# Splitting the delta rule's output into stages and putting attention scores and projections between them

## The reference, cut to what matters

```python
def gated_delta_rule(q, k, v, g, beta):          # 4 heads of 128, run here on blocks of 128 tokens
    a_mat = strict_lower(kbeta @ k.T * decay) + I
    u, w = solve(a_mat, [v * beta, kbeta * exp(g)])
    attn = lower(q @ k.T * decay)
    for n in blocks:                             # state starts at 0
        v_new = u_n - w_n @ state
        o_n = (q_n * exp(g_n)) @ state + attn_n @ v_new
        state = state * exp(g_last) + (k_n * exp(g_last - g_n)).T @ v_new

o_a = rmsnorm(gated_delta_rule(...)) * silu(gz)
o_b = softmax(causal(qf @ kf.T * scale)) @ vm * silu(mz)      # 8 heads, 192 wide, two at a time
x = x + concat([o_a, o_b, o_c]) @ w_out
```

## Time and profile before

| what | value |
|---|---|
| median of three executions | 1759.2 us |
| profiled execution | 1756.48 us, span 1754.7 us |
| PE busy | 1661.3 us, 95% |
| VectorE busy | 1048.1 us, 60% |
| ScalarE busy | 872.9 us, 50% |
| mean granted TensorE clock | 0.974 of full |
| HBM traffic | 253.24 MB, 144 GB/s on average |

### The profile page before, as it was taken

The page is one execution under the profiler, slowest core; times in us unless marked ns, Lnnn a source line. Parts: engine busy times, 40 slices in busy tenths (PEclk is TensorE's granted clock), DMA queues, the critical chain, the costliest instruction groups (busy, mean ns, idle before and its releaser), DMA issues.

```text
span 1754.7 us, 27203 instructions
## 1 busy us (share of the span) xinstructions
PE 1661.3 (95%) x11578; PEld 1531.1 (87%) x11578; DVE 1048.1 (60%) x1506; ACT 872.9 (50%) x1297; POOL 97.7 (6%) x72
## 2 busy tenths in 40 slices
PE   7999899999989899999888999999999998789999
PEld 7989777989977799999887899989999997679998
DVE  6875564896646555555786645455646465555554
ACT  4975363686445435435445533344454357443332
POOL 0112000012200000000240000000000000000000
PEclk9999999999999899999999999998999999899999
DMA  7624224552313465555321555544665553035552
GB/s 224 191 66 135 71 73 145 157 158 89 97 49 117 163 213 191 171 190 169 121 83 62 168 186 179 188 140 135 196 204 175 185 169 120 24 113 179 190 192 97
DMA packets 204297, 253.24 MB, mean 144 GB/s; under 512 B 17808, under 2 KB 183952, under 8 KB 204048
## 3 DMA queue, kind: packets, MB, share of 16 engines
q1 hardware_dynamic: 204176, 251.49, 44.9%
HBM read 250.43 MB, written 1.05 MB: 143 GB/s over the span
## 4 chain that ended last, share of the span: by engine, by line
PE 78%; DVE 8%; ACT 6%; issue 5%; DMA 1%; POOL 1%; SPq 0%; DVEq 0%; ACTq 0%; POOLq 0%
PE bank L784 77%; ACT arena L1377 4%; DVE weights_rest L1889 2%; ACT weights_high L1377 1%; PE bank L842 1%; DVE arena L2036 1%; DMA ring<-in_w_in 1%; ACT L1377 1%; ACT L1372 1%; DVE small L2206 0%; DVE x L2252 0%; DVE weights_rest_more L1889 0%; DVE arena L2224 0%; POOL arena L2520 0%; DMA vec<-in_vec 0%
## 5 line engine op out<-in xcount | busy, mean ns | idle before, releaser
L784 PE MATMUL bank<-xT_high,weights_high 128*128 128x256 f32 (+1 forms) x2352 | 676.1, 288 | 8.9 <-DVE weights_rest L1889 4.1
L784 PE MATMUL bank<-xT_rest,weights_high 128*128 128x256 f32 (+1 forms) x2352 | 658.3, 284 | 0.0
L784 PE MATMUL bank<-xT_high,weights_rest 128*128 128x256 f32 (+1 forms) x2048 | 581.4, 285 | 0.0
L1889 DVE TENSOR_TENSOR weights_rest<-ring,weights_high 128x1024 fp32r<-128x1024 f32 (+3 forms) x414 | 486.6, 1225 | 98.8 <-ACT weights_high L1377 95.1
L1377 ACT ACTIVATE weights_high<-ring 128x1024 fp32r<-128x1024 f32 (+3 forms) x414 | 400.6, 1019 | 253.9 <-PE bank L784 235.6
L784 PEld LDWEIGHTS bank<-xT_high,weights_high 128*128 128x128 f32 (+1 forms) x2352 | 454.2, 193 | 19.4 <-issue 8.9
L784 PEld LDWEIGHTS bank<-xT_rest,weights_high 128*128 128x128 f32 (+1 forms) x2352 | 448.1, 192 | 3.5 <-issue 2.0
L784 PEld LDWEIGHTS bank<-xT_high,weights_rest 128*128 128x128 f32 (+1 forms) x2048 | 395.7, 193 | 0.6
L1377 ACT ACTIVATE arena<-bank 128x512 f32<-128x512 f32 (+4 forms) x253 | 134.5, 547 | 390.3 <-PE bank L784 327.4
L784 PE MATMUL bank<-arena 128*128 128x128 f32 (+2 forms) x1416 | 209.4, 307 | 37.3 <-ACT arena L1377 22.9
L784 PEld LDWEIGHTS bank<-arena 128*128 128x128 f32 (+1 forms) x1416 | 180.2, 203 | 63.6 <-ACT arena L1377 22.6
(11 more groups left out here) (180 smaller groups left out, 1698.1 us busy)
## 6 DMA issues: line engine op xcount, KB each, us to landing
ring<-in_w_in SPq DMA_DIRECT2D x36, 1024.0 KB, 5.2
ring<-in_ffn_w_gate SPq DMA_DIRECT2D x36, 1024.0 KB, 5.4
ring<-in_ffn_w_up SPq DMA_DIRECT2D x35, 1024.0 KB, 5.4
ring<-in_ffn_w_down SPq DMA_DIRECT2D x34, 1024.0 KB, 4.9
ring<-in_w_out SPq DMA_DIRECT2D x22, 1024.0 KB, 4.9
ring<-in_w_in_a SPq DMA_DIRECT2D x11, 1024.0 KB, 5.2
ring_more<-in_ffn_w_down SPq DMA_DIRECT2D x10, 1024.0 KB, 5.1
ring_more<-in_ffn_w_up SPq DMA_DIRECT2D x9, 1024.0 KB, 5.3
```

The source lines that it names most:

```text
L784: return eng.matmul(o, a, b, start=first, stop=last)
L1889: TTs(rest_slot(b)[:, part], raw_slot(b)[:, part], high_slot(key)[:, part].bitcast(F32), ALU.subtract).then_inc(*dv.mark(("rest", key, z)))
```

## The change

`gdn_o` is cut into four kinds of stages, and the scores of a pair get a stage `sc` of their own for pairs 0 and 1 (for these, `att` does nothing on PE and only the DVE part is left). The matmuls, evictions and products are the same ones in the same number.

- `gdn_u` l, n: PE u (for n = 1 also w); ACT their evictions.
- `gdn_w` l: PE wS; DVE the subtraction.
- `gdn_o` l, n: PE S (n = 0) and o; ACT the copy of S and the square of o; nothing on DVE.
- `gdn_n` l, n: PE on; ACT logarithm and exponential; DVE the products by norm, gain and gates.

The order in each layer becomes

The diff, cut to its core (the engines' functions are cut along the same lines; `LABEL` only keeps the semaphores' names):

```diff
+LABEL = dict(gdn_u="gdn_o", gdn_w="gdn_o", gdn_n="gdn_o", sc="att")
...
-                  32: (rots[0:3], rots[3:5]), 64: ([proj("mz", 0)], [])}
+                  32: (rots[0:3], rots[3:5]), 64: ([proj("mz", 0)], [("sc", f"m{l}", 0)])}
...
-        out += [("gdn_o", l, 0), ("att", m, 0), ("sm", m, 0), proj("mz", 1), ("gdn_o", l, 1)]
+        out += [("gdn_u", l, 0), ("att", m, 0), ("sm", m, 0), proj("mz", 1), ("gdn_o", l, 0), ("gdn_u", l, 1)]
+        out += [("sc", m, 1), ("gdn_n", l, 0), ("gdn_w", l)]
...
+            if hp == 1:
+                out[-3:] = [("gdn_o", l, 1), ("sm", m, 1), proj("mz", 2), ("gdn_n", l, 1), ("parts", f"h{l}", *ready[1])]
...
+            def st_gdn_w(st):
+                l = st[1]
+                pe.wait_ge(*at(("wT", l)))
+                pe.wait_ge(*at(("St", l)))
+                b = group(("wS", l))
+                for h in range(4):
+                    ins = mm(b[:, h * P:h * P + P], wT[:, h, :], St[:, h, :])
+                ins.then_inc(*pe.mark(("wS", l)))
...
             def st_att(st):
+                if (st[1][0], st[2]) not in (("m", 0), ("m", 1)):
+                    st_sc(st)
+
+            def st_sc(st):
                 _, name, hp = st
```

More of the change, by code:

```diff
@@ L169, in schedule @@
                   8: ([("ukv", l, 0, 0)], [("ukv", l, 0, 1)]), 16: ([("ukv", l, 1, 0)], [("ukv", l, 1, 1)]),
-                  32: (rots[0:3], rots[3:5]), 64: ([proj("mz", 0)], [])}
+                  32: (rots[0:3], rots[3:5]), 64: ([proj("mz", 0)], [("sc", f"m{l}", 0)])}
         out += [("tri", l, 0, 1), ("trid", l, 0, 1), proj("gz", 1), ("tri", l, 1, 1), ("trid", l, 1, 1)]
+        m = f"m{l}"
         for s in LEVELS[1:]:
@@ L174, in schedule @@
                 out += [("tri", l, n, s)] + beside[s][n] + [("trid", l, n, s)]
-        m = f"m{l}"
-        out += [("gdn_o", l, 0), ("att", m, 0), ("sm", m, 0), proj("mz", 1), ("gdn_o", l, 1)]
+        out += [("gdn_u", l, 0), ("att", m, 0), ("sm", m, 0), proj("mz", 1), ("gdn_o", l, 0), ("gdn_u", l, 1)]
+        out += [("sc", m, 1), ("gdn_n", l, 0), ("gdn_w", l)]
         o = ("outp", f"h{l}", 16)
@@ L992, in st_trid, with st_gdn_u @@
                     ins.then_inc(*pe.mark(("D", l, n, s, z)))
-            def st_gdn_o(st):
+            def st_gdn_u(st):
                 _, l, n = st
@@ L1001, in st_gdn_o @@
                 ins.then_inc(*pe.mark(("u", l, n)))
+                if n:
+                    pe.wait_ge(*at(("TTg", l)))
+                    b = group(("w", l))
+                    for h in range(4):
+                        ins = mm(b[:, h * P:h * P + P], ktm[:, 1, h, :], ET[:, 1, h, :])
+                    ins.then_inc(*pe.mark(("w", l)))
+            def st_gdn_w(st):
[3 more added lines that the diff above has]
+                b = group(("wS", l))
+                for h in range(4):
+                    ins = mm(b[:, h * P:h * P + P], wT[:, h, :], St[:, h, :])
+                ins.then_inc(*pe.mark(("wS", l)))
+            def st_gdn_o(st):
+                _, l, n = st
                 if n == 0:
@@ L1009, in st_gdn_o @@
                 else:
[L1010 to L1020, removed]
                     pe.wait_ge(*at(("vn", l, 1)))
@@ L1028, in st_gdn_o, with st_gdn_n @@
                 ins.then_inc(*pe.mark(("o", l, n)))
+            def st_gdn_n(st):
+                _, l, n = st
                 pe.wait_ge(*at(("osq", l, n)))
@@ L1349, in _ @@
             PEX = dict(lru_b=None, lru_c=None, silu=None, decay_b=st_decay_b, vT=st_vT, norm=st_norm, ab=st_ab, abt=st_abt, parts=None, hg_n=st_hg_n, proj=st_proj, lru=st_lru, decay=st_decay, l2=st_l2, mla_norm=st_mla_norm,
-                       gdn_a=st_gdn_a, tri=st_tri, trid=st_trid, gdn_o=st_gdn_o, uq=st_uq, rot=st_rot, ukv=st_ukv, att=st_att, sm=None, hg_diff=None, pv=st_pv,
+                       gdn_a=st_gdn_a, tri=st_tri, trid=st_trid, gdn_u=st_gdn_u, gdn_w=st_gdn_w, gdn_n=st_gdn_n, sc=st_sc, gdn_o=st_gdn_o, uq=st_uq, rot=st_rot, ukv=st_ukv, att=st_att, sm=None, hg_diff=None, pv=st_pv,
                        outp=st_outp, final=None, ffn=st_ffn, norm_front=None, norm_part=st_norm, norm_turn=st_norm, norm_in=None, memkv=st_memkv, memkn=st_memkn, memq=st_memq, pa=st_px, pb=st_px, pk=st_px,
@@ L1355, in _ @@
             for st in sched:
-                pe.stage(st[0], st)
+                pe.stage(LABEL.get(st[0], st[0]), st)
                 if PEX[st[0]]:
@@ L1645, in st_gdn_o, with st_gdn_u, st_gdn_n @@
                 _, l, n = st
+                if n == 0:
+                    copy(St, ("S", l), ps(("S", l), 4, P), ("St", l))
+                g = ("o", l, n)
+                copy(sq[:, n], g, ps(g, 2, S), ("osq", l, n), func=ACT.Square)
+            def st_gdn_u(st):
+                _, l, n = st
                 g = ("u", l, n)
                 copy(U[:, n], g, ps(g, 4, P), ("vn", l, 0) if n == 0 else ("u1", l))
-                if n == 0:
-                    copy(St, ("S", l), ps(("S", l), 4, P), ("St", l))
-                else:
+                if n:
                     copy(wT, ("w", l), ps(("w", l), 4, P), ("wT", l))
-                g = ("o", l, n)
-                copy(sq[:, n], g, ps(g, 2, S), ("osq", l, n), func=ACT.Square)
+            def st_gdn_n(st):
+                _, l, n = st
                 g = ("on", l, n)
@@ L1857, in _ @@
                      norm=st_norm, ab=st_ab, abt=st_abt, parts=st_parts, hg_n=st_hg_n, proj=st_proj, lru=st_lru, decay=st_decay, l2=st_l2, mla_norm=st_mla_norm,
-                     gdn_a=st_gdn_a, tri=st_tri, trid=None, gdn_o=st_gdn_o, uq=st_uq, rot=None, ukv=st_ukv, att=None, sm=st_sm, hg_diff=st_hg_diff, pv=st_pv,
+                     gdn_a=st_gdn_a, tri=st_tri, trid=None, gdn_u=st_gdn_u, gdn_w=None, gdn_n=st_gdn_n, sc=None, gdn_o=st_gdn_o, uq=st_uq, rot=None, ukv=st_ukv, att=None, sm=st_sm, hg_diff=st_hg_diff, pv=st_pv,
                      outp=st_outp, final=st_final, ffn=st_ffn, norm_front=st_norm_front, norm_part=st_norm_back, memkv=st_memkv,
@@ L1865, in _ @@
             for st in sched:
-                ac.stage(st[0], st)
+                ac.stage(LABEL.get(st[0], st[0]), st)
                 if X[st[0]]:
@@ L2148, in st_trid, with st_gdn_w, st_gdn_n @@
                         TTs(ET[:, 1], TT[:, 1, 1], bcast(beg[:, 1, :], P), ALU.mult).then_inc(*dv.mark(("TTg", l)))
-            def st_gdn_o(st):
+            def st_gdn_w(st):
+                l = st[1]
+                dv.wait_ge(*at(("u1", l)))
+                dv.wait_ge(*at(("wS", l)))
+                TTs(U[:, 1], U[:, 1], ps(("wS", l), 4, P), ALU.subtract).then_inc(*dv.mark(("vn", l, 1), frees=("wS", l)))
+            def st_gdn_n(st):
                 _, l, n = st
[L2152 to L2155, removed]
                 g = ("o", l, n)
@@ L2434, in _ @@
                      norm=st_norm, ab=st_ab, abt=st_abt, parts=st_parts, hg_n=st_hg_n, proj=st_proj, lru=st_lru, decay=st_decay, l2=st_l2, mla_norm=st_mla_norm,
-                     gdn_a=st_gdn_a, tri=None, trid=st_trid, gdn_o=st_gdn_o, uq=st_uq, rot=st_rot, ukv=st_ukv, att=st_att, sm=st_sm, hg_diff=st_hg_diff, pv=st_pv,
+                     gdn_a=st_gdn_a, tri=None, trid=st_trid, gdn_u=None, gdn_w=st_gdn_w, gdn_n=st_gdn_n, sc=None, gdn_o=None, uq=st_uq, rot=st_rot, ukv=st_ukv, att=st_att, sm=st_sm, hg_diff=st_hg_diff, pv=st_pv,
                      outp=st_outp, final=st_final, ffn=st_ffn, norm_front=st_norm_front, norm_part=st_norm_back, memkv=st_memkv,
@@ L2441, in _ @@
             for st in sched:
-                dv.stage(st[0], st)
+                dv.stage(LABEL.get(st[0], st[0]), st)
                 if X[st[0]]:
```

## The result

The changed kernel took 1742.57 us (median of four executions, 1740.66 to 1745.49) against 1759.16 us for the kernel before (1757.85 to 1759.99): a ratio of 0.9917, interval 0.9889 to 0.9944. Three later sessions, each on another chip (which one the first ran on is not known), timed the same two programs again. There the changed kernel was where it had been (1743.85, 1743.94, 1742.65 us), but the kernel before was not: 1753.19, 1755.20 and 1753.86 us, from 17, 13 and 17 executions. Within each session the savings are 9.3, 11.3 and 11.2 us (ratios 0.9941, 0.9930 and 0.9935; intervals 0.9928 to 0.9954, 0.9914 to 0.9947, 0.9917 to 0.9953). The first session's interval, 0.9889 to 0.9944, takes in all three ratios; it stands for a saving of anything from 9.9 to 19.5 us.

A forecast was written before the change was run, and what follows sets the result against it. PE, busy 95% of the span, was taken as the bound. Removing 8.8 us and adding 3.4 gave 5.7 us a layer with denser groups; both layers less 2.0 for clock gave 9.4, so 1749.8 us, range 1745 to 1757.

The forecast's parts named there:

- The removed waits: Between proj mz0 and mz3, PE's five waits for ACT and one for DVE's subtraction go: 6.09 us a layer.
- The half clock removed: wS and the second o, behind the 2.42 us wait, return to full clock: 2.7 us a layer saved.
- the bank wait: Inside pv 0, before its second transposes, PE waits 2.3 us until DVE's product by the norm frees o's bank.
- the copies' 0.2 us: Before pv 0's product PE waits some 0.2 us, as ACT copies the transposes only behind block 0's norm.
- The wait of 0.15 for the subtraction: Before the second o PE waits 0.15 us, as DVE's subtraction of wS stands behind the products of gdn_n 0.
- mz2's bank: mz2 needs a bank of scores 1, free near 220.3; PE arrives at 220.45: no cost, margin 0.2 us.
- The two fewer breaks: Two fewer breaks between PE's groups in each layer's stretch, whose pieces overlap by some 0.15 us when dense.
- The clock in the new gap: Behind the new 2.3 us gap in pv 0: half clock in two cases of three, about 1.5 us an event.
- A: Rival: the gap in pv 0 grows, half clock lasts into mz2's start; gain 4 us, 1755 us; chance 0.15.
- B: Rival: each layer's last product is bound by the weight stream, giving the gain back; 1759 us; chance 0.08.
- C: Rival: ACT's queue comes late to scores 1's end and PE waits; slower, 1763 us at 7.6 us late; chance 0.05.
- D: Rival: added waits smaller or clock holds in both layers, 3.4 and 2.0 us less; 1746 or 1743 us; chance 0.14.

The follow-up runs named there:

- the dummies: Kernel before plus 8 useless 128-column matmuls into wS's bank, in the 2.42 us wait ahead of wS, both layers: 1748.47 us against 1753.86, ratio 0.9969.
- block 1 alone: Changed kernel with block 0's u, S, o and norm in one piece again, block 1 still cut and spread: 1746.15 us against 1753.19 for before, ratio 0.9959.

## Why the prediction was wrong in its time and right in its mechanism

**The base failed.** The step was: "The median shown is 2.7 us above it, so I forecast 1759.2 - 9.4 = 1749.8 us." The saving was subtracted from a median of three executions that the program did not keep. In the three later sessions the kernel before had its medians at 1753.2, 1755.2 and 1753.9 us (47 executions, 1747.5 to 1759.3), while the changed kernel kept within 1742.6 to 1743.9. From a base of 1753.9 the same 9.4 us give 1744.5. The range of 12 us held the saving's uncertainty and none of the base's, though the profile at hand (1756.48 us) already lay 2.7 us below the median. Why the first session's four executions all lay above 1757.8 is not settled: neither their clocks nor the chip are known. In the later sessions the five executions above 1757.8 us had a mean clock of 0.970 to 0.975, so more half clock is the likely cause, but that is argued, not shown.

**The removed waits** (6.09 us a layer): right, all six gone in both layers. **The half clock removed** (2.7 us): right to 0.1 us for the profile I read, but 1.2 and 1.6 us in the next profile of the same program. Over the five profiled stretches of the old order, held against the 53.88 us with the dummies, it is 2.1 us on average.

**What is late next**: the bank wait was forecast at 2.3 us and is 2.50, from the chain that was named (norm, DVE product); before pv 1's products 0.85 was forecast and 0.97 came; the copies' 0.2 us came as 0.24 in three of the nine stretches, among them the one where the clock held. The wait of 0.15 for the subtraction does not show. mz2's bank cost nothing. Added in all: 3.6 us where 3.4 was forecast.

**The two fewer breaks** were sized too small; this is the term of the walk that was most off. With the clock at 1.00 in both, the old order takes 53.88 us and the new one 49.90: 3.98 us. Waits removed (6.09 us) less waits added (2.50 + 0.24 + 0.97, of which 0.1 was there before) are 2.5 us of it; the rest, some 1.5 us, is PE's rows lying denser when groups follow without a wait. PE's busy time agrees: 49.4 us less 1.8 for the dummies in the old order, 46.2 in the new, 1.4 us less. I had put it at 0.3.

**The clock in the new gap** was forecast in two cases of three at 1.5 us; it fell in eight of nine at 0.8 to 1.4 us. That is 1.0 us a layer forecast and 0.9 measured.

Sum: 4.7 us a layer forecast. The profiled pair shows 5.65; the mean over all profiled stretches is 56.0 us before (five) and 50.8 after (nine), 5.2 a layer or 10.4 in all, and the three later sessions have 9.3 to 11.3 us. That the forecast 9.4 comes so near is in part luck: the breaks gave 1.2 us a layer more than forecast, the half clock removed 0.6 us less and the added waits took 0.2 us more.

**The signs and the rivals.** mz3 came earlier than I had said: its end moved by 7.30 us in the first layer and 14.37 in the second, where I had 4 to 6 and 8 to 12 for its start, partly because 1.66 us and, up to the second, 3.1 us of the move came from outside the stretches. Of the rivals, A's 4 us, B's 0 and C's loss are excluded; D was nearest in time, but for a reason it did not name: no bank wait was missing. Its times do not follow from its terms either: 3.4 us is for one layer, and without 6.8 us of waits and 2.0 us of clock the forecast would be 1741.0 us.

The table load's 1.28 us with 0.02 us behind it showed again (210.43, then 211.73). A drain of 1380 ns behind each load (the Trainium skill, ScalarE: Activation LUTs, What ACT_TABLE_LOAD costs) would have made the bank wait 3.9 us; 2.50 was measured, so this case does not show it.

## What to carry to other kernels

Walk a new order through every in-order queue and through the rotation of the PSUM banks: here the order removed six waits and the one it made was a bank held by a late reader, which one swap in the list took away for another 2.5 us a layer by the stretches and 1.9 by the times. Compare kernels by a stretch between two fixed instructions before you compare their times: where the clock held, the lengths repeated to 0.2 us between layers (53.88 and 53.89, 48.15 and 48.32, 47.45 and 47.46), while the time of one program moved by 12 us. Read the mean clock of each execution beside its time. And do not hang a forecast of half a percent on a median of three executions.

## What the runs showed of the hardware

PE idle for 2.4 us cost a second time here: with eight useless matmuls in each of the two waits the kernel was 5.4 us faster, and the 0.63 us left idle was not followed by half clock. Half clock also followed an idle time of 1.98 us, in both layers of the kernel with block 1 alone. How much half clock costs depends on when it comes: in the same program it covered wS and o (2.6 us) or a part of o alone (1.2 us). And the time before the first stretch, in which all these programs are the same, ended at 187.8 to 188.9 us in nine profiles and at 189.8 to 190.2 us in four; what parts the two groups is not settled.
